# A modulation vector gathered as rows by one product of 512 columns in each feed-forward pass

## The chip, the cores and the metric

The kernel runs on one core of a Trainium2 chip. Its engines are TensorE (PE in the profile), VectorE (DVE), ScalarE (ACT), GpSimd (POOL) and SyncE (SP), which here only issues transfers. The metric is the device time of one execution in microseconds; the median of three runs is given. All times below are in us unless marked ns.

## The reference

Two transformer blocks follow each other on 256 tokens of width 1024. What touches the change:

```python
# first block (twice, around a mixer)
h = h + 0.5 * ((silu(gate) * up) @ w_out)        # gate, up = split(rmsnorm(h) @ w_in); D_FF = 2816
# second block
c_act = silu(c)                                   # c: [1, 1024]
mod = c_act @ w_ada + b_ada                       # w_ada: [1024, 6144]
shift1, scale1, gate1, shift2, scale2, gate2 = split(mod, 6)
h = rms_norm(x, g_pre_mix) * (1.0 + scale1) + shift1
```

The vector `mod` depends on `c` alone. The kernel computes most of it during the two feed-forward stages of the first block, long before it is used.

## The kernel before

**The passes.** Each feed-forward stage (`ffn1`, `ffn2`) goes through its 2816 hidden channels in 11 steps of 256, ten passes of a loop and an end. A pass of TensorE is a wide slab for the gate (48 products of 128x256), a wide slab for the up part (48), and a deep slab (48 products that add to banks 0 to 3). Every weight slab is 128x2048 floats (1 MB), fetched by SyncE into `raw` (three slots). ScalarE copies it into `wh` at reduced precision (the weight copies one, two and three of a pass), and VectorE writes the rest, `raw - wh`, into `wl` (split one, two and three). Three products, `wh` with the high part, `wh` with the low part, `wl` with the high part of the input, make one exact product. Between them VectorE reads the gate bank and the up bank, ScalarE applies the curve (silu), VectorE multiplies, ScalarE rounds the hidden values (`fh`) and VectorE takes their low part (`fl`).

**The modulation.** In each pass one step of 256 of the 6144 columns of `mod` is computed: SyncE fetches 1 MB of `w_ada` into `ada_raw` (L547), GpSimd multiplies it by `c_act` (L692) and folds it three times, 2048 to 1024 to 512 to 256 columns (L695, L697, L701, the last into `ada_sum`). TensorE sums over the partitions by `modulate` (L2175): for each half of `ada_sum` a product with one column of ones, which puts 128 values into one column of bank 7. Ten steps fall into `ffn1`, ten into `ffn2` (`ADA_EARLY` = 20), four into the last stage.

**What sets the order.** Each engine runs its own program in order; semaphores order them among each other. SyncE waits with the fetch of step n for `ada_free`, the third fold of step n-1, and this wait stands ahead of the slabs of the next pass in its queue. TensorE waits for `ada_free` at the end of a pass. Behind `modulate` stands a product of zeros over the gate bank (`long_zeros`, L2151), whose values the next slab's first product overwrites; behind that the loop branches.

At the end of `ffn2` VectorE reads the 40 columns of bank 7 in `modulation_vectors` (L1383 to L1393) and then adds the four banks of the deep slabs to the residual (L1456). ScalarE squares those for the next norms (L1070).

## Time and profile before

| | |
|---|---|
| median of 3 runs | 1006.28 us (1006.11 to 1006.47) |
| the profiled execution | 1004.26 us |
| its span | 1002.4 us, 18812 instructions |
| busy: PE, PEld, DVE, ACT, POOL | 97%, 92%, 78%, 50%, 51% |
| mean traffic | 190 GB/s |

The profile is one execution on the chip. PE's busy share holds modelled ends of pipelined products, so starts are read rather than lengths: 48 products of 256 columns in 5.44 us are 0.113 each, whatever the 278 ns of one record. A VectorE or GpSimd record that is longer than others of its form contains time in which it was blocked after it had been started. In rows of a timeline the bracket gives the idle time before an operation and what ended it.

### The profile page before, as it was taken

The numbers are of one execution on the slowest core, as the hardware profiler recorded it, in microseconds if no ns is written. First come the engines' busy times: TensorE is split into PE (matmuls) and PEld (weight loads), VectorE is DVE, ScalarE is ACT, GpSimd is POOL, SyncE is SP. The second block draws the span as 40 slices with busy tenths as digits, with TensorE's granted clock in tenths as the row PEclk, the third lists the DMA queues.
The fourth block names the chain that finished last, engine by engine and source line by source line (L and its number), as shares of the span: only waits on it lengthen the run. The fifth ranks groups of instructions, "written<-read, shape, count | busy, mean of one in ns | idle before, by whom it ended". The sixth has DMA issues, their size and how long they took to land.

```text
span 1002.4 us, 18812 instructions
## 1 busy us (share of the span) xinstructions
PE 975.8 (97%) x7645; PEld 926.8 (92%) x7645; DVE 779.9 (78%) x810; ACT 501.8 (50%) x587; POOL 511.0 (51%) x302
## 2 busy tenths in 40 slices
PE   9999999999989999999999999999989989999997
PEld 8999999998979899999999999978979979999996
DVE  5776565799995679887787779998978887768764
ACT  7433433477541474434334756667657454343432
POOL 4575767610054037577577699999940104314400
PEclk9999999999998999999999999999989999999999
DMA  8966858747360277686776475572236517675641
GB/s 270 360 211 227 275 194 276 242 129 211 96 198 8 84 224 244 232 270 209 261 241 213 140 194 159 142 216 85 85 109 204 193 50 245 228 247 195 216 161 43
DMA packets 166494, 190.06 MB, mean 190 GB/s; under 512 B 10654, under 2 KB 155628, under 8 KB 166316
## 3 DMA queue, kind: packets, MB, share of 16 engines
q1 hardware_dynamic: 165580, 186.13, 57.1%
q0 software_dynamic: 688, 3.07, 1.1%
q8 instruction: 36, 0.59, 0.2%
q10 hardware_dynamic: 176, 0.15, 0.1%
q14 instruction: 14, 0.11, 0.0%
HBM read 187.17 MB, written 2.16 MB: 189 GB/s over the span
## 4 chain that ended last, share of the span: by engine, by line
PE 73%; DVE 15%; POOL 4%; issue 3%; ACT 2%; SPq 1%; DMA 1%; ACTq 0%; DVEq 0%; POOLq 0%
PE ps L2079 46%; PE ps L2123 11%; PE ps L2131 9%; DVE wl L1348 5%; DVE ps L1756 2%; POOL work L825 2%; POOL con L822 2%; PE ps L2364 1%; PE ps L2310 1%; ACT wh L856 1%; PE ps L2175 1%; SPq L564 1%; POOL work L818 1%; PE ps L2151 1%; PE ps L2235 1%
## 5 line engine op out<-in xcount | busy, mean ns | idle before, releaser
L2079 PE MATMUL ps<-xh,wh 128*128 128x256 f32 x1208 | 340.1, 282 | 6.4 <-DVE work L1375 3.2
L2079 PE MATMUL ps<-xl,wh 128*128 128x256 f32 x1208 | 335.4, 278 | 0.0
L2079 PE MATMUL ps<-xh,wl 128*128 128x256 f32 x1208 | 335.2, 278 | 0.0
L1353 DVE TENSOR_TENSOR wl<-raw,wh 128x2048 fp32r<-128x2048 f32 x78 | 231.5, 2968 | 67.4 <-ACT wh L862 67.1
L2079 PEld LDWEIGHTS ps<-xh,wh 128*128 128x128 f32 x1208 | 228.1, 189 | 12.3 <-issue 7.1
L2079 PEld LDWEIGHTS ps<-xl,wh 128*128 128x128 f32 x1208 | 227.8, 189 | 0.5
L2079 PEld LDWEIGHTS ps<-xh,wl 128*128 128x128 f32 x1208 | 227.5, 188 | 0.0
L862 ACT ACTIVATE wh<-raw 128x2048 fp32r<-128x2048 f32 x78 | 149.9, 1922 | 138.3 <-PE ps L2079 101.4
L1348 DVE TENSOR_TENSOR wl<-raw,wh 128x2048 fp32r<-128x2048 f32 (+1 forms) x72 | 181.5, 2527 | 32.7 <-ACT wh L856 32.0
L692 POOL TENSOR_TENSOR ada_raw<-ada_raw,c_act 128x2048 f32<-128x2048 f32 x24 | 90.6, 3775 | 206.5 <-DMA ada_raw<-in_w_ada 201.3
L856 ACT ACTIVATE wh<-raw 128x2048 fp32r<-128x2048 f32 (+1 forms) x74 | 139.5, 1889 | 59.4 <-PE ps L2079 42.3
L2079 PE MATMUL ps<-yh,wh 128*128 128x256 f32 x480 | 135.7, 283 | 1.2 <-DVE work L1884 0.7
L2079 PE MATMUL ps<-yh,wl 128*128 128x256 f32 x480 | 133.6, 278 | 0.0
L2079 PE MATMUL ps<-yl,wh 128*128 128x256 f32 x480 | 133.5, 278 | 0.0
L2079 PEld LDWEIGHTS ps<-yh,wh 128*128 128x128 f32 x480 | 90.8, 189 | 4.3 <-issue 2.0
L2079 PEld LDWEIGHTS ps<-yl,wh 128*128 128x128 f32 x480 | 91.0, 190 | 0.1
L2079 PEld LDWEIGHTS ps<-yh,wl 128*128 128x128 f32 x480 | 90.7, 189 | 0.0
L2123 PE MATMUL ps<-fh,wl 128*128 128x256 f32 x320 | 88.5, 277 | 0.0
L2123 PE MATMUL ps<-fh,wh 128*128 128x256 f32 x320 | 88.5, 276 | 0.0
L2123 PE MATMUL ps<-fl,wh 128*128 128x256 f32 x320 | 88.5, 276 | 0.0
L695 POOL TENSOR_TENSOR ada_raw<-ada_raw 128x1024 f32<-128x1024 f32 x24 | 82.3, 3427 | 1.9
L697 POOL TENSOR_TENSOR ada_raw<-ada_raw 128x512 f32<-128x512 f32 x24 | 72.4, 3016 | 1.9
(426 smaller groups left out, 1773.0 us busy)
## 6 DMA issues: line engine op xcount, KB each, us to landing
raw<-in_ffn_w_in SPq DMA_DIRECT2D x43, 1024.0 KB, 7.6
ada_raw<-in_w_ada SPq DMA_DIRECT2D x24, 1024.0 KB, 5.1
raw<-in_ffn_w_out SPq DMA_DIRECT2D x22, 1024.0 KB, 6.5
raw<-in_w_in SPq DMA_DIRECT2D x18, 1024.0 KB, 5.3
raw<-in_w_mlp_in SPq DMA_DIRECT2D x16, 1024.0 KB, 5.5
raw<-in_w_mlp_out SPq DMA_DIRECT2D x16, 1024.0 KB, 4.9
raw<-in_w_mix_in SPq DMA_DIRECT2D x14, 1024.0 KB, 5.4
raw<-in_w_mix_out SPq DMA_DIRECT2D x4, 1024.0 KB, 5.2
```

Of the source, the lines that this page charges most:

```text
L692: pool.tensor_tensor(ada_raw[:, :, :], ada_raw[:, :, :], c_act[:, :].unsqueeze(2).to_broadcast([P, KT, 256]), ALU.mult).then_inc(S("ada_pa ...
L695: pool.tensor_tensor(flat[:, 0:1024], flat[:, 0:1024], flat[:, 1024:2048], ALU.add).then_inc(S("ada_part"), 1)
L697: pool.tensor_tensor(flat[:, 0:512], flat[:, 0:512], flat[:, 512:1024], ALU.add).then_inc(S("ada_part"), 1)
L822: ins = pool.tensor_scalar(tap_own[:, n, :], upad[:, t, k:k + T], tap(k, t), 0.0, ALU.mult, ALU.add)
L825: ins = pool.tensor_tensor(sums, sums, tap_own, ALU.add)
L856: act.activation(wh[:, s % SLOTS, 0:n], raw[:, s % SLOTS, 0:n], ACT.Copy).then_inc(high_done, 1)
L862: act.activation(wh[:, s % SLOTS, :], raw[:, s % SLOTS, :], ACT.Copy).then_inc(high_done, 1)
L1348: dve.tensor_tensor(wl[:, s % SLOTS, 0:n], raw[:, s % SLOTS, 0:n], wh[:, s % SLOTS, 0:n].bitcast(F32), ALU.subtract).then_inc(low_done, 1)
L1353: dve.tensor_tensor(wl[:, s % SLOTS, :], raw[:, s % SLOTS, :], wh[:, s % SLOTS, :].bitcast(F32), ALU.subtract).then_inc(low_done, 1)
L2079: mm = pe.matmul(bank[:, m * T:(m + 1) * T], w[:, k, m * P:(m + 1) * P], r[:, k, :], start=(m == 0 and k == 0 and j == 0), stop=(k == KT - ...
L2123: mm = pe.matmul(ps[m // 2][:, (m % 2) * T:(m % 2 + 1) * T], w[:, k, m * P:(m + 1) * P], r[:, k, :], start=(begin and k == 0 and j == 0 an ...
L2131: mm = pe.matmul(ps[n][:, :], r[:, k, tk * P:(tk + 1) * P], w[:, k, half * 512:(half + 1) * 512], start=False, stop=stop, skip_group_check ...
```

## The change

- **Rows instead of columns.** TensorE no longer turns each step into two columns. The step's 256 sums per partition are split into a high part and a low part that stand next to each other (`ada_parts`, 128x512). One product with `step_pick` as weights (128x20, a single column of ones, at the step's place) adds the partition sums to row n of bank 7 and zeros to the 19 others. The bank is cleared once, in `ffn1`. The product of zeros at the end of each pass is gone.
- **GpSimd** folds into another buffer (`ada_fold`: `at_mat` in the first stage, part of `w_v` in the second), then waits for ScalarE and subtracts the high part (128x256). `ada_free` is now this subtraction.
- **ScalarE** makes `step_pick` (128x20) and the high part (128x256) in `high_sum`, which stands between the curve and weight copy two and waits for the third fold.
- **SyncE** waits with the next fetch for the first fold only.
- **At the end of `ffn2`** VectorE copies the 20 rows out, TensorE turns them in `turn_rows` after four of the eight tiles of the last deep slab, and VectorE adds the two parts by reading strided columns in `modulation_vectors`.
- The memset of `qkvp`'s pads moves from the start of GpSimd's program to behind its first loop, since `ada_parts` lies over it. The last stage keeps the old steps (`modulation_late`, `modulate_late`).

TensorE at the end of a loop pass of `ffn1`, before (L2123 is the deep slab, L2175 `modulate`, L2151 the zeros; two records of a small product are one row here):

```order
L2123 MATMUL ps<-fh,wl 128x256
L2175 ISA [waits s_ada_free]
L2175 MATMUL ps<-con,ada_sum 128x1
L2175 ISA
L2175 MATMUL ps<-con,ada_sum 128x1
L2222 REGISTER_ALU
L2151 MATMUL ps<-zero 128x512 [waits s_hidden_gate]
L2226 REGISTER_ALU
L2226 COMPARE_AND_BRANCH
```

The same place after the change (L2168 is the deep slab, L2295 the last one behind the loop):

```order
L2168 MATMUL ps<-fh,wl 128x256
L2219 MATMUL ps<-yl,step_pick 20x512 [waits s_ada_free]
L2286 REGISTER_ALU
L2286 COMPARE_AND_BRANCH
L2295 MATMUL ps<-yl,wh 128x256 [waits low_done,s_hidden_low]
```

Three products and their register work give way to one product, and the wait for `ada_free` stands before it.

ScalarE in a loop pass of `ffn1`, before (L862 the weight copies one, two and three, L891 the curve, L895 the rounding):

```order
L862 ACTIVATE wh<-raw 128x2048 [waits taken]
L890 REGISTER_ALU
L891 ACTIVATE hid<-hid 128x512 [waits s_hidden_gate]
L860 REGISTER_ALU
L861 REGISTER_ALU [waits slot0_loaded]
L862 ACTIVATE wh<-raw 128x2048 [waits taken]
L907 REGISTER_ALU
L895 ACTIVATE fh<-hid 128x512 [waits s_hidden,taken]
L862 ACTIVATE wh<-raw 128x2048 [waits taken,slot1_loaded]
```

And after (L890 the weight copies, L919 the curve, L923 the rounding, L929 and L930 the new ones):

```order
L890 ACTIVATE wh<-raw 128x2048 [waits taken]
L918 REGISTER_ALU
L919 ACTIVATE hid<-hid 128x512 [waits s_hidden_gate]
L928 ISA [waits s_ada_taken]
L929 ISA [waits s_ada_part]
L929 ACTIVATE step_pick<-step_line 128x20
L930 ACTIVATE yl<-work 128x256
L888 REGISTER_ALU
L889 REGISTER_ALU [waits slot0_loaded]
L890 ACTIVATE wh<-raw 128x2048 [waits taken]
L944 REGISTER_ALU
L923 ACTIVATE fh<-hid 128x512 [waits s_hidden,taken]
```

Two waits and two operations have moved in ahead of weight copy two, the rounding and weight copy three.

The diff, cut to its core:

```diff
@@ sync
-            def modulation(step):
-
-                if not isinstance(step, int) or step:
+            def modulation(step, late=False):
+
+                if late:
                     sp.wait_ge(*at("ada_free", step))
+                elif not isinstance(step, int) or step:
+                    sp.wait_ge(*at("ada_part", step * 5 - 3))
@@ gpsimd
+            def modulation(step, name):
+                flat = ada_raw[:, :, :].rearrange("p k m -> p (k m)")
+                fold, parts = ada_fold[name], ada_parts[name]
+                pool.wait_ge(*at("ada_loaded", step * 16 + 16))
+                pool.tensor_tensor(ada_raw[:, :, :], ada_raw[:, :, :], c_act[:, :].unsqueeze(2).to_broadcast([P, KT, 256]),
+                                   ALU.mult).then_inc(S("ada_part"), 1)
+                pool.wait_ge(*at("ada_part", step * 5 + 1))
+                pool.tensor_tensor(fold[:, :], flat[:, 0:1024], flat[:, 1024:2048], ALU.add).then_inc(S("ada_part"), 1)
...
+                pool.tensor_tensor(fold[:, 0:256], fold[:, 0:256], fold[:, 256:512], ALU.add).then_inc(S("ada_part"), 1)
+                pool.wait_ge(*at("ada_part", step * 5 + 5))
+                pool.tensor_tensor(parts[:, 1, :], fold[:, 0:256], parts[:, 0, :].bitcast(F32), ALU.subtract)\
+                    .then_inc(S("ada_free"), 1)
...
+            pool.wait_ge(*at("ada_taken", FF_STEPS - 1))
+            pool.memset(qkvp[:, :, 0:3], 0.0).then_inc(S("pads"), 1)
@@ scalar, ffn
+                def high_sum(step):
+                    if not isinstance(step, int) or step:
+                        act.wait_ge(*at("ada_taken", step))
+                    act.wait_ge(*at("ada_part", step * 5 + 4))
+                    act.activation(step_pick[:, :], step_line[:, bass.ds(step * -1 + (ADA_EARLY - 1), ADA_EARLY)], ACT.Copy)
+                    act.activation(ada_parts[name][:, 0, :], ada_fold[name][:, 0:256], ACT.Copy).then_inc(S("ada_part"), 1)
...
                     silu(i + 2)
+                    high_sum(i + first)
                     cast_in_loop(s + 4, i, 3, 1)
@@ vector, modulation_vectors
                 dve.wait_ge(*at("ada_taken", ADA_EARLY))
+                dve.tensor_copy(ada_rows, ps[7][0:ADA_EARLY, :]).then_inc(S("ada_rows"), 1)
...
+                dve.wait_ge(*at("ada_cols", 1))
...
-                st(dve.tensor_tensor(ada[:, 0:n], ps[7][:, 0:n], vec[:, g * P + r:g * P + r + n], ALU.add))
+                st(dve.tensor_tensor(by_half(ada[:, 0:n]), ps[7][:, 0:n].rearrange("p (m s) -> p m s", m=2),
+                                     by_half(vec[:, g * P + r:g * P + r + n]), ALU.add))
@@ tensor
-            def modulate(step):
+            def modulate(step, name):
+
+                pe.wait_ge(*at("ada_free", step + 1))
+                pe.matmul(ps[7][0:ADA_EARLY, :], step_pick[:, :], ada_parts[name].rearrange("p a t -> p (a t)"), start=False, stop=False, skip_group_check=True)\
+                    .then_inc(S("ada_taken"), 1)
...
+            def turn_rows():
+
+                pe.wait_ge(*at("ada_rows", 1))
+                for half in range(2):
+                    for part in range(2):
+                        mm = pe.matmul(ps[7][:, half * ADA_EARLY:(half + 1) * ADA_EARLY],
+                                       ada_rows[:, part * T + half * P:part * T + (half + 1) * P], ident[0:ADA_EARLY, 0:ADA_EARLY],
+                                       start=(half == 0 and part == 0), stop=(part == 1), skip_group_check=True)
+                mm.then_inc(S("ada_cols"), 1)
@@ tensor, ffn
                     pe.wait_ge(*at("x_in", 4))
+                    long_zeros(ps[7])
                     wide(s0 + 1, up_bank, high, low)
...
-                    modulate(i + (0 if name == "ffn1" else FF_STEPS - 1))
-                    pe.wait_ge(*at(name + "_gate", i + 2))
-                    long_zeros(gate_bank)
+                    modulate(i + (0 if name == "ffn1" else FF_STEPS - 1), name)
...
+                    if name == "ffn2" and m == 3:
+                        turn_rows()
```

## Rows read from the trace of the kernel before

**Rows 1.** Page, part 4: the chain that ended last, by engine.

```profile
PE 73%; DVE 15%; POOL 4%; issue 3%; ACT 2%; SPq 1%; DMA 1%; ACTq 0%; DVEq 0%; POOLq 0%
```

**Rows 2.** Stretches A:B: length, busy PE, PEld, DVE, ACT, POOL, PEclk, DMA, GB/s.

```profile
113.00:130.40 17.40, 17.40 (x150) 16.99 (x150) 11.30 (x7) 6.80 (x6) 11.91 (x4) 1.00 0.71 241
428.70:445.90 17.20, 17.20 (x150) 16.96 (x150) 14.62 (x7) 6.96 (x6) 11.69 (x5) 1.00 0.70 233
```

**Rows 3.** Chain in order of time: start us, us, what.

```profile
43.08 11.10 PE ps L2079 x96
...
124.07 5.44 PE ps L2123 x48
129.51 0.58 PE ps L2175 x4
130.09 0.32 PE ps L2151
...
200.06 5.66 PE ps L2235 x48
...
411.17 0.32 PE ps L2151
...
828.21 5.49 PE ps L2131 x24
```

**Rows 4.** Timeline of PE, ffn2, boundary of a pass: start us, us, what.

```profile
479.44 0.50 PE L2175 MATMUL ps<-con,ada_sum 128*128 128x1 f32 x4
479.87 0.38 PE L2151 MATMUL ps<-zero 1*128 1x512 bf16 x1
480.19 0.38 PE L2079 MATMUL ps<-yh,wh 128*128 128x256 f32 x1
480.41 0.28 PE L2079 MATMUL ps<-yl,wh 128*128 128x256 f32 x1
```

**Rows 5.** Timeline of PE at the loop branch of the last stage.

```profile
855.47 0.50 PE L2175 MATMUL ps<-con,ada_sum 128*128 128x1 f32 x4
...
856.03 0.28 PE L2079 MATMUL ps<-xl,wh 128*128 128x256 f32 x1
```

**Rows 6.** Timeline of POOL, one pass of ffn2.

```profile
427.89 3.61 POOL L692 TENSOR_TENSOR ada_raw<-ada_raw,c_act 128x2048 f32<-128x2048 f32 x1 [5.18 <-DMA ada_raw<-in_w_ada]
431.57 2.73 POOL L695 TENSOR_TENSOR ada_raw<-ada_raw 128x1024 f32<-128x1024 f32 x1
434.38 3.22 POOL L697 TENSOR_TENSOR ada_raw<-ada_raw 128x512 f32<-128x512 f32 x1
437.68 2.67 POOL L701 TENSOR_TENSOR ada_sum<-ada_raw 128x256 f32<-128x256 f32 x1
```

**Rows 7.** Timeline of DVE, the same pass.

```profile
428.72 3.32 DVE L1415 TENSOR_TENSOR fl<-hid,fh 128x512 fp32r<-128x512 f32 x1 [1.25 <-ACT fh L895]
431.96 4.49 DVE L1353 TENSOR_TENSOR wl<-raw,wh 128x2048 fp32r<-128x2048 f32 x1
...
441.78 2.29 DVE L1353 TENSOR_TENSOR wl<-raw,wh 128x2048 fp32r<-128x2048 f32 x1 [1.27 <-ACT wh L862]
```

**Rows 8.** Timeline of SyncE (SPq) and POOL; page, part 6: median to landing.

```profile
402.58 0.37 SPq L541 DMA_DIRECT2D raw<-in_ffn_w_out  x1
...
410.23 3.61 POOL L692 TENSOR_TENSOR ada_raw<-ada_raw,c_act 128x2048 f32<-128x2048 f32 x1 [7.23 <-DMA ada_raw<-in_w_ada]
...
ada_raw<-in_w_ada SPq DMA_DIRECT2D x24, 1024.0 KB, 5.1
```

**Rows 9.** ScalarE's copies by line: busy us, mean ns, idle before.

```profile
L862 ACT ACTIVATE wh<-raw 128x2048 fp32r<-128x2048 f32 x78 | 149.9, 1922 | 138.3 <-PE ps L2079 101.4
...
L1260 ACT ACTIVATE xh<-work 128x256 fp32r<-128x256 f32 x8 | 3.4, 419 | 0.3
```

**Rows 10.** Timeline of DVE and ACT, end of ffn2.

```profile
550.71 0.69 DVE L1456 SCALAR_TENSOR_TENSOR resid<-ps,resid 128x512 f32<-128x512 f32 x1
...
555.62 0.91 ACT L1070 ACTIVATE work<-resid,att_col 128x256 f32<-128x256 f32 x2 [0.46 <-DVE resid L1456]
```

More of the change, by code:

```diff
@@ L447, in two_blocks @@
         y_eps, z_eps, scale_m = kr, kr_raw, ps[6][:, T:2 * T]
+        ada_fold = {"ffn1": at_mat, "ffn2": w_v[:, 0:1024]}
+        ada_parts = {"ffn1": yl[:, 0:2, :], "ffn2": xh[:, 4:6, :]}
+        ada_rows = w_kn[0:ADA_EARLY, 0:512]
         gate_row, z_rows, z_junk = w_qn[:, 0:D], w_kn, w_v
@@ L663, in _ @@
                     deep(s + 1 + i * 6, s + 1, "w_mlp_out_2", i * 3 + r)
-                modulation(i + ADA_EARLY)
+                modulation(i + ADA_EARLY, late=True)
             for k in range(ADA_MLP * SLOTS + 1, MLP_STEPS):
@@ L684, in _, with modulation_late @@
             pool.memset(zero[:, :], 0.0).then_inc(S("zero"), 1)
-            pool.memset(qkvp[:, :, 0:3], 0.0).then_inc(S("pads"), 1)
+            ps_(pool.memset(step_line[:, :], 0.0))
+            ps_.sync()
+            pool.memset(step_line[:, ADA_EARLY - 1:ADA_EARLY], 1.0).then_inc(S("pads"), 1)
             pool.memset(mpad[:, :, 0:2], 0.0).then_inc(S("pads"), 1)
-            def modulation(step):
+            def modulation(step, name):
[6 more added lines that the diff above has]
+                pool.tensor_tensor(fold[:, :], flat[:, 0:1024], flat[:, 1024:2048], ALU.add).then_inc(S("ada_part"), 1)
+                pool.wait_ge(*at("ada_part", step * 5 + 2))
+                pool.tensor_tensor(fold[:, 0:512], fold[:, 0:512], fold[:, 512:1024], ALU.add).then_inc(S("ada_part"), 1)
+                pool.wait_ge(*at("ada_part", step * 5 + 3))
+                pool.tensor_tensor(fold[:, 0:256], fold[:, 0:256], fold[:, 256:512], ALU.add).then_inc(S("ada_part"), 1)
+                pool.wait_ge(*at("ada_part", step * 5 + 5))
+                pool.tensor_tensor(parts[:, 1, :], fold[:, 0:256], parts[:, 0, :].bitcast(F32), ALU.subtract)\
+                    .then_inc(S("ada_free"), 1)
+            def modulation_late(step):
                 flat = ada_raw[:, :, :].rearrange("p k m -> p (k m)")
@@ L693, in modulation @@
                                    ALU.mult).then_inc(S("ada_part"), 1)
-                pool.wait_ge(*at("ada_part", step * 3 + 1))
+                pool.wait_ge(*at("ada_part", step * 3 + 1 + 2 * ADA_EARLY))
                 pool.tensor_tensor(flat[:, 0:1024], flat[:, 0:1024], flat[:, 1024:2048], ALU.add).then_inc(S("ada_part"), 1)
-                pool.wait_ge(*at("ada_part", step * 3 + 2))
+                pool.wait_ge(*at("ada_part", step * 3 + 2 + 2 * ADA_EARLY))
                 pool.tensor_tensor(flat[:, 0:512], flat[:, 0:512], flat[:, 512:1024], ALU.add).then_inc(S("ada_part"), 1)
-                pool.wait_ge(*at("ada_part", step * 3 + 3))
-                if not isinstance(step, int) or step:
-                    pool.wait_ge(*at("ada_taken", step))
+                pool.wait_ge(*at("ada_part", step * 3 + 3 + 2 * ADA_EARLY))
+                pool.wait_ge(*at("ada_taken", step))
                 pool.tensor_tensor(ada_sum[:, :], flat[:, 0:256], flat[:, 256:512], ALU.add).then_inc(S("ada_free"), 1)
@@ L716, in _ @@
             pool.wait_ge(low_done, 3)
-            modulation(0)
+            modulation(0, "ffn1")
             pool.dma_start(con[:, N_CONST_FIRST:N_CONST], a["table"][:, N_CONST_FIRST:]).then_inc(S("con_rest"), 16)
@@ L722, in _ @@
             with pool.Fori(0, FF_STEPS - 2) as i:
-                modulation(i + 1)
+                modulation(i + 1, "ffn1")
+            pool.wait_ge(*at("ada_taken", FF_STEPS - 1))
+            pool.memset(qkvp[:, :, 0:3], 0.0).then_inc(S("pads"), 1)
             def add_pairs(n, ready, src, pairs=range(4)):
@@ L784, in _ @@
             with pool.Fori(0, FF_STEPS - 1) as i:
-                modulation(i + (FF_STEPS - 1))
+                modulation(i + (FF_STEPS - 1), "ffn2")
+            pool.wait_ge(*at("ada_free", ADA_EARLY))
             pool.wait_ge(*at("pos_loaded", 16))
@@ L840, in _ @@
             with pool.Fori(0, ADA_MLP) as i:
-                modulation(i + ADA_EARLY)
+                modulation_late(i + ADA_EARLY)
         @block.scalar
@@ L895, in round_hidden @@
                     act.activation(high[:, :, :], pair(hid[:, 3, :]), ACT.Copy).then_inc(S(name + "_fh"), 1)
+                def high_sum(step):
[4 more added lines that the diff above has]
+                    act.activation(ada_parts[name][:, 0, :], ada_fold[name][:, 0:256], ACT.Copy).then_inc(S("ada_part"), 1)
+                first = 0 if name == "ffn1" else FF_STEPS - 1
                 cast(s0 + 3)
@@ L912, in ffn @@
                 silu(FF_STEPS)
+                high_sum(first + FF_STEPS - 2)
                 round_hidden(FF_STEPS, last_high[name])
@@ L1489, in _ @@
             s0 = FIRST["mix"]
-            dve.wait_ge(*at("pads", 2))
+            dve.wait_ge(*at("pads", 3))
             dve.wait_ge(*at("con_rest", 16))
```

11 lines of the change are left out of this document (8 added, 3 removed).

## The prediction

> **What bounds the kernel now.** I read the chain of waits by engine first. TensorE (PE) carries 73% of it [rows 1], so the question is what TensorE does at the place of the change, and for whom it waits there. Next the stretches of one feed-forward pass (first stage: ffn1, second: ffn2): PE is busy in all of it at the full granted clock, VectorE (DVE) 11.30 us of 17.4 in the first stage and 14.62 us of 17.2 in the second, ScalarE (ACT) under 7, GpSimd (POOL) some 11.9, the DMA engines 0.7 [rows 2]. Then the chain in order of time. A pass is 96 products of the two wide slabs (11.10 us), 48 of the deep slab (5.44), the four small modulation products and one product of zeros [rows 3]. In the first stage the small products take 0.58 and the zeros 0.32. From 43.08 to 200.06 there are nine passes of 17.44 on average (first stage); from the wide start at 411.49 (the end of the zeros) to 480.19 four of 17.18 (second stage) [rows 3, 4]. So the second stage is paced by PE alone, the first waits some 0.25 a pass for GpSimd: its loop of transfer, four vector operations and "free" closes just when the deep slab ends.
>
> **The boundary of a pass.** In the timeline of PE the small products start at 479.44, the zeros 0.43 later, the next wide product 0.32 after that, and its successor 0.22 later instead of the usual 0.113 (5.44 over 48). From 479.44 to 480.41, less one normal spacing, that is 0.86 us without useful streaming, in each of 20 passes [rows 3, 4].
>
> **What the change removes and adds on PE.** It takes away the four small products (0.43) and the zeros (0.43 with the bubble behind them) and puts in one product of 512 columns. A 512-column product of the same type streams in 5.49/24 = 0.23 [rows 3]. For the bubble behind it (the loop branch stands there) I bound from both sides: none, or the same 0.20 as behind the zeros. The last stage of the kernel has the same small products directly before its branch: from 855.47 to 856.03 less one spacing is 0.45, which is the small products alone with no bubble to speak of [rows 5]. There the products last 0.43, here the cover is 0.23, so I take 0.20: boundary 0.43, saving 0.43 a pass. Bounds of the boundary: 0.23 to 0.64. A pass paced by PE alone is then 16.54 + 0.23 + 0.20, about 16.77.
>
> The Trainium skill's page "Runtime: NRT & Kernel Launch", section on instruction fetch mechanics, says that a taken branch to a target outside the fetched window must refetch and stalls. The row of the last stage shows no such stall behind 0.43 of cover; by the rule it could show behind 0.23. That is the upper bound 0.64 and the fourth case below.
>
> **GpSimd's work and the copy of its input.** A step keeps its multiply and three folds, and gains a subtraction of 256 columns. The first fold now writes elsewhere, so the next input may be fetched as soon as that fold is done; SyncE comes to it right behind the deep slab's transfer, no longer at the end of the pass. That transfer follows split three: after the deep slab's end a rounding (about 0.6), copy three (1.92) and the split (2.29), so about 4.8 into a pass [rows 7, 9]. Today the modulation's fetch lands 5.1 after its issue (the median), and 7.65 after the deep slab's issue when it goes behind it (402.58 to 410.23) [rows 8]. From 4.8 this gives 12.5 into the pass, where it was 4.2 into the next (5.1 less the 0.9 of the boundary). So the wait of the first stage's passes for GpSimd should go, unless something else is late. What would be late is the port.
>
> **The operations of VectorE and GpSimd exclude each other.** In the rows of one pass DVE's low part of the hidden values (own time 0.54) is asked for at 428.72 and ends at 432.04, after GpSimd's multiply ended at 431.50. GpSimd's first fold ends at 434.30, DVE's split of a slab, asked for at 431.96, at 436.45, GpSimd's second fold, asked for at 434.38, at 437.60 [rows 6, 7]. From one end to the next the own times are 3.61, 2.26 and 1.15 for POOL, and by halving 0.6 for the third fold; 0.54 and 2.15 for DVE. The readings of PSUM by DVE take no part. Sum a pass now: POOL 7.6, DVE 3 x 2.15 + 2 x 0.54 = 7.5, together 15.1 of 17.19. After: one more operation of 0.6, together 15.7 of 16.77. 1.0 us stays free, and both engines would have to be there to use the rest. They are not: the fold must go through ScalarE before GpSimd can subtract (a copy of 256 columns is 0.42 [rows 9], with the small one of the picking column, estimated at 0.1 by its 20 columns, and two hops some 0.6), and DVE waits about 1.2 a pass for copy three and as much for the rounding [rows 7].
>
> The Trainium skill's page "SBUF — State Buffer", section "SBUF: two separate sides", has this as a lock held for the whole instruction between GpSimd and VectorE operations with two SBUF inputs. By the rule the added subtraction costs VectorE time although GpSimd has idle time (case one); if it did not hold, the sum would be that of case two. The rows agree with the rule.
>
> **What ScalarE's new place costs.** The two copies stand between the curve and weight copy two and wait for the third fold. If GpSimd starts its multiply at 12.5, then with today's total of 12.15 for four contended operations (427.89 to 440.35 with gaps, less 0.3) [rows 6] the third fold ends at 24.6, which is 7.9 into the next pass, before the curve is through (in the pass from 428.7 the first split ends at 436.45 [rows 7], and a reading and the curve follow: 9). No block. But a multiply at 12.5 stands in front of DVE's split of slab two (asked for at 13): that ends at 18.2, the hidden product behind the first fold at 20.9, the rounding, copy three and split three follow at 21.5, 23.4 and 25.7, so 8.9 into the next pass instead of 4.7. The deep slab's fetch is issued there, and the modulation's behind it lands at 16.6 instead of 12.5. The third fold is then through at 12 into the following pass, copy two waits for it (0.9 late), and the subtraction, contended at 2.67, ends at 15.3, only 1.2 before PE asks. One more collision of 1.9 makes PE wait 0.7. Queued behind a waiting high sum are copy two, the rounding and copy three, and behind these DVE's splits.
>
> So the period lies between 16.77 (never late) and 18.1 (POOL's contended 12.15 + 2.67 + 0.6, with hops 15.5, plus the 2.6 that the fetch loses behind the deep slab's, each pass). I take 17.1: one late pass in two, 0.7 each, which is 0.33 on the average.
>
> **The sum.** First stage: nine passes from 17.44 to 17.1, 3.1; its first pass, in which nothing contends, 0.4. Second stage: ten passes from 17.19 to 17.1, 0.9. Added once: a product of zeros for bank 7 at the start, 0.35 [rows 3], and the turn of the rows in the last deep slab. For the turn DVE copies 20x512 (0.69 by its first residual sum, which reads as many columns [rows 10], beside PE's work), PE runs 4 products in two parts each, 8 x 0.11 = 0.9 [rows 4], at 2.7 into the slab, and DVE's modulation vectors wait for it with the residual sums behind them. The first residual sum was at 550.71 [rows 10]; now the turn ends at 552.8, the vectors at 553.6. With residual sums of 0.6 and ScalarE's squares of 0.87 a pair the last square ends at about 558.0 where it was 556.53 [rows 10]: 1.5, less part of what the earlier boundary gives, 1.4. Bounds 0.9 (PE's time alone) to 2.5 (all of the delay of the first sum). GpSimd's later work starts earlier or as before: nothing. The memset of the pads falls in GpSimd's idle time behind the last pass. Total: 3.1 + 0.4 + 0.9 - 0.35 - 1.4 = 2.7 faster. The profiled execution takes 1004.26 (span 1002.4); so 1001.6 for it, and against the median 1006.28, which is 2.0 above the profiled one, 1003.6.
>
> **The rivals.**
> - *Two, the port is no matter* (17%): all passes at 16.77. Nine times 0.67, 0.4, ten times 0.42, less 1.75: 8.9 faster, 997.4. For it: today's second stage loses nothing at 15.1 of 17.19. Against: DVE is blocked there for 2 to 2.8 us at a time.
> - *Three, slower* (23%): the late pass feeds on itself. Place: ScalarE's high sum holds copy two, so split two meets the next multiply. It decides once the subtraction ends more than 16.5 into its pass, from a fetch landing about 17.8. At a period of 17.5: first stage 9 x 0.06 lost, second 10 x 0.31 lost, 1.75 lost, 0.4 won: 5.0 slower, 1011.3. At 18.1 it would be 16 slower.
> - *Four, a bubble behind the product* (10%): boundary 0.64, period 16.98, port harmless: 4.1 + 0.4 + 2.1 - 1.75 = 4.9 faster, 1001.4.
> - *Five, it comes to nothing* (15%): period 17.2 from here and there a late pass; 2.2 + 0.4 - 0.1 - 1.75 = 0.8 faster, 1005.5.
>
> **Chances.** My forecast 35%, its own range 1001.3 to 1005.6 (periods 17.0 to 17.2). A measurement of this kernel tells 0.2%, 2.0 us, from no change. Faster: 60% of mine, two, four, a little of five: 0.50. Slower: 0.24. Same: 0.26. The range reaches into two and three: 997.0 to 1010.5.
>
> **What would show it.** PE's boundary: small products and zeros gone, one 512-column product, the next wide product 0.3 to 0.5 behind its start. GpSimd: multiply 10 to 17 into a pass, no wait for the transfer of some 5 in each pass of the first stage. DVE's busy time up from 11.3 to over 13 in the first stage. ScalarE waiting for GpSimd at the high sum in some passes, none in others. PE waiting for GpSimd's subtraction in some passes: if in none and the passes are 16.8, case two. In the tail the first residual sum some 2.5 later. I am wrong if the passes lengthen everywhere, or if PE waits for a slab's low part instead of the subtraction.

## The result and the profile after

The changed kernel takes 1012.39 (median of 5 runs, 1008.33 to 1015.71), the kernel before 1006.14 beside it (5 runs, 1005.99 to 1006.47): a ratio of 1.0064, 95% interval 1.0044 to 1.0084. It is slower, by more than the 0.2% that can be told apart, and lies above my range. The profiled execution took 1008.33, its span is 1006.5.

Part 4 of its page, by engine, against [rows 1]:

```profile
PE 40%; POOL 24%; DVE 15%; issue 14%; ACT 4%; DMA 1%; POOLq 0%; ACTq 0%; DVEq 0%
```

TensorE no longer carries the chain. A pass is counted here from the start of the one product of 512 columns (L2219) to the next. The boundary itself is better than forecast. Timeline of PE in ffn2 (start us, us, what), against [rows 4]:

```profile
425.01 0.28 PE L2168 MATMUL ps<-fh,wl 128*128 128x256 f32 x1
425.12 0.39 PE L2219 MATMUL ps<-xh,step_pick 128*20 128x512 f32 x1
425.36 0.28 PE L2124 MATMUL ps<-yh,wh 128*128 128x256 f32 x1
```

The next wide product starts 0.24 behind the product of 512 columns, without a bubble: 0.86 of [rows 3, 4] has become 0.24, not 0.43. But only eleven of the eighteen passes between the boundaries have the period that this gives, 16.56. The other seven take 17.17 to 20.68; in ffn1 they come every second time from the fifth pass on, in ffn2 from the third. Here are three passes in a row, against [rows 2] (length, busy PE, PEld, DVE, ACT, POOL, granted clock, DMA share, GB/s):

```profile
109.50:128.10 18.60, 16.90 (x148) 16.62 (x147) 16.64 (x8) 7.28 (x8) 11.81 (x5) 1.00 0.50 168
128.10:144.60 16.50, 16.50 (x147) 16.46 (x145) 11.68 (x7) 6.44 (x7) 12.64 (x5) 1.00 0.92 300
144.60:163.60 19.00, 17.16 (x148) 16.58 (x148) 17.19 (x8) 8.00 (x8) 14.30 (x5) 1.00 0.55 183
```

The clock is full in all three, so these late passes are waits. Of the seven only the longest (180.2 to 200.8, the last of ffn1) has a fall of the clock in it: 0.57 in 194 to 198, in part at the lower level of 1.2 GHz, which is worth some 1.7 of its 20.68 (0.43 of these 4.0). The list of waits (engine, line, for whom: us in total, times, longest):

```profile
ACT step_pick L929 <- POOL work L709: 37.0, 8, 5.3
PE ps L2168 <- DVE wl L1391: 11.1, 7, 1.9
```

ScalarE's high sum waits eight times for GpSimd's third fold, up to 5.3. TensorE waits seven times, as often as there are late passes, and it waits at the deep slab (L2168) for split three (L1391). It does not wait for the subtraction.

**One late pass, link by link** (109.5 to 128.1). ScalarE: the curve L919, the high sum L929 and L930, weight copy two L890, the rounding L923, then copy three:

```profile
101.46 0.63 ACT L919 ACTIVATE hid<-hid 128x512 f32<-128x512 f32 x1 [0.70 <-DVE hid L1413]
107.34 0.22 ACT L929 ACTIVATE step_pick<-step_line 128x20 fp32r x1 [5.25 <-POOL work L709]
...
107.78 1.90 ACT L890 ACTIVATE wh<-raw 128x2048 fp32r<-128x2048 f32 x1
117.69 0.64 ACT L923 ACTIVATE fh<-hid 128x512 fp32r<-128x512 f32 x1 [8.01 <-DVE hid L1456]
118.23 1.90 ACT L890 ACTIVATE wh<-raw 128x2048 fp32r<-128x2048 f32 x1
```

ScalarE was through the curve at 102.1. Copy two has to wait for TensorE to leave its slab, which comes 11.4 into a pass (the first experiment shows it), here at 104.4; it starts at 107.78, held 3.4 by the high sum. GpSimd: third fold, then multiply and first fold of the next step, then the multiply after that:

```profile
106.47 0.74 POOL L709 TENSOR_TENSOR work<-work 128x256 f32<-128x256 f32 x1
...
109.04 3.61 POOL L702 TENSOR_TENSOR ada_raw<-ada_raw,c_act 128x2048 f32<-128x2048 f32 x1 [0.35 <-DMA ada_raw<-in_w_ada]
112.73 4.32 POOL L705 TENSOR_TENSOR work<-ada_raw 128x1024 f32<-128x1024 f32 x1
...
130.89 3.61 POOL L702 TENSOR_TENSOR ada_raw<-ada_raw,c_act 128x2048 f32<-128x2048 f32 x1 [5.02 <-DMA ada_raw<-in_w_ada]
```

VectorE: split two, the hidden product, split three:

```profile
109.71 5.08 DVE L1391 TENSOR_TENSOR wl<-raw,wh 128x2048 fp32r<-128x2048 f32 x1 [3.88 <-ACT wh L890]
114.72 2.88 DVE L1456 TENSOR_TENSOR hid<-hid 128x512 f32<-128x512 f32 x1
...
120.17 2.29 DVE L1391 TENSOR_TENSOR wl<-raw,wh 128x2048 fp32r<-128x2048 f32 x1 [0.86 <-ACT wh L890]
```

Split two comes to VectorE at 109.71, 0.67 after GpSimd's next multiply has started, and takes 5.08 where [rows 7] had 4.49 and its own time is some 2.2. The hidden product behind it takes 2.88 instead of 0.68, because GpSimd's first fold has got in ahead. So the rounding comes at 117.69 and split three ends at 122.46. TensorE at the deep slab:

```profile
120.54 0.28 PE L2124 MATMUL ps<-xh,wl 128*128 128x256 f32 x1
122.51 0.39 PE L2168 MATMUL ps<-fh,wh 128*128 128x256 f32 x1 [1.70 <-DVE wl L1391]
```

And SyncE's queue (L546 the deep slab's fetch, L554 the modulation's):

```profile
101.01 0.37 SPq L546 DMA_DIRECT2D raw<-in_ffn_w_out  x1
103.25 0.37 SPq L554 DMA_DIRECT2D ada_raw<-in_w_ada  x1
...
122.64 0.37 SPq L546 DMA_DIRECT2D raw<-in_ffn_w_out  x1
123.30 0.37 SPq L554 DMA_DIRECT2D ada_raw<-in_w_ada  x1
```

In the pass before, the modulation's fetch went out at 103.25, with the first fold. In the late pass the first fold ended at 117.05, but the fetch stands behind the deep slab's, which has to wait for split three: it goes out at 123.30, 6.2 later, and the multiply starts at 130.89. So the third fold is late again when ScalarE comes to the high sum in the next pass, and everything repeats: one pass in phase, one late. The place of the collision changes a little. In the late pass from 144.6 split two gets in just ahead of the multiply and takes 2.29, the hidden product is held instead (4.09), and then split three (3.39); TensorE waits 1.7 there too.

**Where 4.1 of span went**, from the first wide or deep product behind a boundary to the next such place, both kernels:

| stretch | before | after | difference | forecast |
|---|---|---|---|---|
| start to the first boundary | 43.01 | 43.49 | +0.5 | -0.05 |
| nine passes of ffn1 | 156.98 | 157.58 | +0.6 | -3.1 |
| mixer | 194.23 | 191.16 | -3.1 | 0 |
| nine passes of ffn2 | 154.74 | 156.88 | +2.1 | -0.9 |
| last boundary to glu's wide slab | 12.65 | 16.47 | +3.8 | +1.4 |
| the rest | 440.8 | 440.9 | +0.1 | 0 |

The +0.6 of ffn1 holds the 1.7 of the clock; the waits alone would have left that stage 1.1 shorter than before.

The tail of ffn2 on VectorE and PE (the copy of the 20 rows, the turn, the bias, the first two residual sums), against [rows 10]:

```profile
552.83 0.67 DVE L1423 COPY work<-ps 20x512 f32<-20x512 f32 x1
554.65 0.20 DVE L1431 TENSOR_TENSOR ada<-ps,vec 128x40 f32<-128x40 f32 x1 [1.16 <-PE ps L2241]
...
555.55 0.69 DVE L1501 SCALAR_TENSOR_TENSOR resid<-ps,resid 128x512 f32<-128x512 f32 x1
```
```profile
553.55 1.06 PE L2241 MATMUL ps<-con,work 20*128 20x20 f32 x8 [1.44 <-DVE work L1423]
```

### The profile page after: what moved, and what is told of

Its sections match the earlier page's. It is cut to its first block, busy times and chain, and to the rows that moved or that the text cites. A ratio compares the mean times of both kernels' runs of the same rounds, so it can differ in the third digit from the quotient of the medians.

```text
span 1006.5 us, 18735 instructions
## 1 busy us (share of the span) xinstructions
PE 966.5 (96%) x7574; PEld 918.7 (91%) x7574; DVE 812.4 (81%) x811; ACT 508.9 (51%) x627; POOL 525.1 (52%) x324
## 4 chain that ended last, share of the span: by engine, by line
PE 40%; POOL 24%; DVE 15%; issue 14%; ACT 4%; DMA 1%; POOLq 0%; ACTq 0%; DVEq 0%
PE ps L2124 23%; PE ps L2176 9%; POOL ada_raw L702 6%; POOL work L705 6%; DVE wl L1386 5%; POOL work L707 4%; POOL work L709 3%; POOL work L853 2%; DVE ps L1801 2%; POOL con L850 2%; ACT wh L884 1%; PE ps L2426 1%; ACT wh L890 1%; DMA raw<-in_ffn_w_in 1%; PE ps L2372 1%
## 5 line engine op out<-in xcount | busy, mean ns | idle before, releaser
L1391 DVE TENSOR_TENSOR wl<-raw,wh 128x2048 fp32r<-128x2048 f32 x78 | 244.0, 3129 | 61.1 <-ACT wh L890 60.1
L890 ACT ACTIVATE wh<-raw 128x2048 fp32r<-128x2048 f32 x78 | 148.3, 1909 | 66.7 <-PE ps L2124 61.3
L702 POOL TENSOR_TENSOR ada_raw<-ada_raw,c_act 128x2048 f32<-128x2048 f32 x20 | 74.9, 3747 | 53.0 <-DMA ada_raw<-in_w_ada 47.9
L2168 PE MATMUL ps<-fh,wh 128*128 128x256 f32 x320 | 89.9, 281 | 11.1 <-DVE wl L1391 11.1
L2168 PE MATMUL ps<-fh,wl 128*128 128x256 f32 x320 | 89.3, 279 | 0.0
L2168 PE MATMUL ps<-fl,wh 128*128 128x256 f32 x320 | 89.2, 279 | 0.0
L705 POOL TENSOR_TENSOR work<-ada_raw 128x1024 f32<-128x1024 f32 x20 | 73.4, 3672 | 1.6
L755 POOL TENSOR_TENSOR work<-work 128x256 f32<-128x256 f32 x13 | 12.8, 990 | 113.9 <-ACT work L907 55.0
```

The lines of the kernel that those rows point to most:

```text
L702: pool.tensor_tensor(ada_raw[:, :, :], ada_raw[:, :, :], c_act[:, :].unsqueeze(2).to_broadcast([P, KT, 256]), ALU.mult).then_inc(S("ada_pa ...
L705: pool.tensor_tensor(fold[:, :], flat[:, 0:1024], flat[:, 1024:2048], ALU.add).then_inc(S("ada_part"), 1)
L890: act.activation(wh[:, s % SLOTS, :], raw[:, s % SLOTS, :], ACT.Copy).then_inc(high_done, 1)
L1391: dve.tensor_tensor(wl[:, s % SLOTS, :], raw[:, s % SLOTS, :], wh[:, s % SLOTS, :].bitcast(F32), ALU.subtract).then_inc(low_done, 1)
L2168: mm = pe.matmul(ps[m // 2][:, (m % 2) * T:(m % 2 + 1) * T], w[:, k, m * P:(m + 1) * P], r[:, k, :], start=(begin and k == 0 and j == 0 an ...
```

## The experiments

On this trace three theories stood against each other. P, the place: the high sum holds copy two, so VectorE's splits slip into GpSimd's multiply. F, the fetch: the modulation's fetch is held behind the deep slab's, which waits for the split that slipped. L, the load: the added subtraction fills the port shared by VectorE and GpSimd. P and F were taken as rivals; the first two results together say that both are links of one: **the late pass is a loop through several queues**, and a cut at either link ends it. A fourth possibility, tested last, is that the tail slows the kernel. Each ratio is to the kernel before, run beside it on the same chip.

**The high sum behind weight copy two.**

```diff
-                    high_sum(i + first)
                     cast_in_loop(s + 4, i, 3, 1)
+                    high_sum(i + first)
```

> The changed kernel, with ScalarE's two high-sum copies behind weight copy two instead of ahead of it (in the loop passes; the last pass as it was). Theory P (place): in every second pass ScalarE waited for the third fold (5.25 us at 107.34) with copy two behind it, and so split two met the next multiply; then the late passes go, all passes are 16.6 to 17.0 and the time is 998 to 1002. Rival F (fetch): the lateness comes from the modulation's fetch, which stands behind the deep slab's in SyncE's queue, so a late split three makes the next multiply late wherever the high sum stands; then passes of 18.5 to 19 stay at every second place and the time is 1006 to 1014. Rival L (load): the fifth vector operation fills the port that VectorE and GpSimd share; as F, 1006 to 1014.

999.27 (996.53 to 1003.48), ratio 0.9919 (0.9889 to 0.9949). ScalarE in a pass of ffn2, and its wait:

```profile
432.90 1.92 ACT L890 ACTIVATE wh<-raw 128x2048 fp32r<-128x2048 f32 x1 [1.32 <-PE ps L2124]
434.73 0.20 ACT L929 ACTIVATE step_pick<-step_line 128x20 fp32r x1
```
```profile
ACT step_pick L929 <- POOL work L709: 8.7, 3, 3.2
```

Copy two starts when its slab has come free, the high sum behind it is mostly ready (8.7 of waiting in three passes instead of 37.0 in eight), and PE has no wait for a slab's low part in the two stages. That is as P expected, and F and L had the late passes stay. Fourteen of the eighteen passes take 16.56 to 16.66. The place has a price of its own in the first pass (18.14): there TensorE waits 1.4 for the subtraction. The others are 17.03 and two of 17.2 to 17.3 at a slower pace, of which the last section tells.

**The modulation's fetch ahead of the deep slab's.**

```diff
-                    deep(s + 2 + i * 3, s + 2, w_out, i + (start - 1))
                     modulation(i + (1 if name == "ffn1" else FF_STEPS))
+                    deep(s + 2 + i * 3, s + 2, w_out, i + (start - 1))
```

> The changed kernel, with the modulation's fetch issued ahead of the deep slab's in each loop pass of SyncE instead of behind it. Theory F: the fetch no longer waits for split three, lands some 3 to 5 us earlier, no multiply starts late, the late passes go: 998 to 1003. Theory P: ScalarE still holds copy two whenever the third fold is late, but the fold is late less often: some late passes stay, 1003 to 1009. Theory L: the load of the port is the same, 1006 to 1014.

997.99 (993.0 to 1002.35), ratio 0.9887 (0.9838 to 0.9936). SyncE and GpSimd in a pass of ffn2:

```profile
428.12 0.37 SPq L554 DMA_DIRECT2D ada_raw<-in_w_ada  x1
433.56 0.37 SPq L546 DMA_DIRECT2D raw<-in_ffn_w_out  x1
```
```profile
423.62 4.33 POOL L705 TENSOR_TENSOR work<-ada_raw 128x1024 f32<-128x1024 f32 x1
...
435.13 1.64 POOL L711 TENSOR_TENSOR xh<-work,xh 128x256 fp32r<-128x256 f32 x1 [4.33 <-ACT xh L930]
436.73 3.60 POOL L702 TENSOR_TENSOR ada_raw<-ada_raw,c_act 128x2048 f32<-128x2048 f32 x1
```

The fetch goes out 0.2 after the first fold's end, and the multiply starts right behind the subtraction, in the same place of each pass. The high sum stays where the change put it and, but for one wait of 2.8, holds nothing: periods of 16.56 to 17.19, no late pass. P had expected some late passes to stay (1003 to 1009). So one link cut is enough. In a second run on another chip the same kernel took 998.9, ratio 0.993 (0.9905 to 0.9955):

> The changed kernel with the modulation's fetch issued ahead of the deep slab's, once more, beside the next two on one chip. By the head-of-line theory no late pass (periods 16.57 to 17.2, no wait of TensorE for a slab's low part) and 0.4 to 1.3% faster than before. From the last boundary product to glu's first wide product 15.9, as in its first profile.

Again no late pass (16.5 to 17.2), and the tail from the last boundary's product takes 16.1.

**Without the low part.** No subtraction, one product of 256 columns, so this kernel's modulation has only reduced precision. GpSimd's wait for ScalarE's copy moves to the start of its next step.

```diff
-                pool.wait_ge(*at("ada_part", step * 5 + 5))
-                pool.tensor_tensor(parts[:, 1, :], fold[:, 0:256], parts[:, 0, :].bitcast(F32), ALU.subtract)\
-                    .then_inc(S("ada_free"), 1)
...
-                pe.matmul(ps[7][0:ADA_EARLY, :], step_pick[:, :], ada_parts[name].rearrange("p a t -> p (a t)"), ...
+                pe.matmul(ps[7][0:ADA_EARLY, 0:T], step_pick[:, :], ada_parts[name][:, 0, :], ...
```

> The changed kernel without GpSimd's subtraction: the low part of the modulation's sums is left out, and the product takes 256 columns (the high part alone). GpSimd still waits for ScalarE's copy before the next multiply. Theory L: 0.6 us of port time and a collision of up to 1.9 us go in each pass, so the late passes go: 998 to 1002 with passes of 16.5. Theories P and F: the third fold is as late as before relative to its fetch, late passes stay but are shorter by 0.7 to 2: 1003 to 1009.

1014.35 (1010.63 to 1019.1), ratio 1.0056 (1.0027 to 1.0086): no better than the change itself, far from the 998 to 1002 of L and above the 1003 to 1009 expected by P and F. Its waits (each line number is one lower here, GpSimd's folds two higher):

```profile
ACT step_pick L928 <- POOL work L711: 45.1, 9, 5.5
PE ps L2167 <- DVE wl L1390: 11.3, 7, 1.9
```

Again seven late passes, of 18.1 to 19.2 (five of the others are at 17.08 instead of 16.44, the slower pace). The subtraction isn't what makes them, and my ledger of the port, in which it was the one new entry, could not have shown them: the order of the queues makes them.

**The fetch held to the end of the step**, as before the change, with the high sum ahead of copy two:

```diff
-                    sp.wait_ge(*at("ada_part", step * 5 - 3))
+                    sp.wait_ge(*at("ada_free", step))
```

> The changed kernel, but SyncE waits with each modulation fetch for the subtraction of the step before (as the kernel before waits for its last fold), so each multiply starts 4 to 5 us into a pass and the third fold ends near 16.5. Theory P (place): ScalarE then holds copy two in every pass, not in every second, until about 16.5, and split three comes near its need: late passes everywhere, 17.5 to 19 each, 1010 to 1030. Against it: if only the collision of split two with the multiply matters, the multiply at 4 to 5 does not meet it, and the passes are 16.6 to 17.2: 997 to 1006.

1043.4 (1035.93 to 1044.73), ratio 1.036 (1.0315 to 1.0404). Waits:

```profile
ACT step_pick L929 <- POOL work L709: 95.2, 18, 6.8
PE ps L2219 <- POOL yl L711: 12.6, 9, 2.1
PE ps L2219 <- POOL xh L711: 10.7, 8, 2.0
```

Now the high sum waits in every pass, all passes but one take 18.6 to 19.6, and TensorE does wait for the subtraction, up to 2.1. The time is above the 1010 to 1030 expected, and what paces it is not only the place of the high sum. GpSimd's subtraction and next multiply, and SyncE:

```profile
483.21 0.73 POOL L711 TENSOR_TENSOR xh<-work,xh 128x256 fp32r<-128x256 f32 x1 [0.74 <-ACT xh L930]
489.88 3.60 POOL L702 TENSOR_TENSOR ada_raw<-ada_raw,c_act 128x2048 f32<-128x2048 f32 x1 [5.94 <-DMA ada_raw<-in_w_ada]
```
```profile
484.11 0.37 SPq L554 DMA_DIRECT2D ada_raw<-in_w_ada  x1
```

The fetch goes out 0.2 behind the subtraction, the multiply starts when it has landed, and the next subtraction ends at 503.49, 19.55 after the one before: a closed loop of transfer, folds, ScalarE's copy and subtraction, longer than a pass of TensorE. So this run doesn't price the place alone. It shows what the early fetch is worth, and one thing more: copy two is held in every pass, yet TensorE waits nowhere for a slab's low part, since split two (484.96) is through before the multiply. The hold needs the collision to make a late pass. And where TensorE had idled ahead of the product, the next wide product starts 0.56 to 0.64 behind it, not 0.24; whether that is the branch no run tells.

**Both cures**, and both with a moved tail (the turn behind the last deep slab's end, the modulation's vectors behind the residual sums):

> Both cures together: the changed kernel with the high sum behind weight copy two and the modulation's fetch ahead of the deep slab's. If place and fetch are two links of one loop (late third fold, late copy two, split two behind the multiply, late split three, late fetch, late third fold), then either cut is enough and both together give little more: passes of 16.57, ratio to the kernel before 0.987 to 0.992, as each alone. If they are two causes that add, each alone would have left late passes that the other takes, and the ratio falls below 0.985.

1000.65 (996.18 to 1004.36), ratio 0.9951 (0.9928 to 0.9975), no wait of PE for a low part in the two stages. Two cures bring no more than one, so they don't add: they cut the same loop. The ratio is even above the expected 0.987 to 0.992; in the trace seven of the eighteen passes are at the slower pace (17.2 to 17.3), which may be a part of it; whether the other executions have them is not shown.

```diff
-                    if name == "ffn2" and m == 3:
-                        turn_rows()
                 mm.then_inc(taken, 1)
+                if name == "ffn2":
+                    turn_rows()
@@ vector
                 if name == "ffn2":
+                    modulation_rest()
                     sub(s + 2)
```

> As the one before, and the rows are turned behind the last deep slab instead of in its middle; VectorE makes the modulation vectors behind its four residual sums instead of ahead of them (the copy of the rows stays ahead). In the changed kernel the first residual sum stood behind the turn. If that is what the end of the second stage costs, 1.5 to 2.5 us come back against the kernel with both cures; if the turn is hidden anyway, nothing, and if the vectors now delay the first scaled input, it loses up to 0.8.

998.14 (992.69 to 1006.66), ratio 0.9937 (0.9906 to 0.9968). From the last boundary's product to glu's first wide product it takes 14.15, against 15.4 with both cures alone. The total's gain of 0.14% lies inside the intervals. (Besides what is shown, TensorE waits at its next sums in bank 7 until the vectors have been read; so in the next two kernels.)

**The moved tail on one cure, and on the changed kernel.**

> The same with the turn of the modulation's rows behind the last deep slab and the modulation's vectors behind the residual sums of the second stage. By the profile of the kernel with both cures and this tail (14.15 from the last boundary product to glu's first wide product, against 15.4 without it) 1.2 to 1.8 us faster than the one without, a ratio lower by 0.0012 to 0.0018. If the tail were hidden anyway, the two would be equal.

994.41 (993.1 to 997.09), ratio 0.9895 (0.9871 to 0.9919), beside 0.993 (0.9905 to 0.9955) for the same without the tail; the tail takes 14.8 against 16.1. That is the 1.3 expected; the ratio's step of 0.0035 is more, but the intervals overlap. The vectors now stand behind the residual sums and delay none:

```profile
541.89 0.67 DVE L1423 COPY work<-ps 20x512 f32<-20x512 f32 x1
542.49 1.27 DVE L1508 SCALAR_TENSOR_TENSOR resid<-ps,resid 128x512 f32<-128x512 f32 x2
...
546.77 0.19 DVE L1438 TENSOR_TENSOR ada<-ps,vec 128x40 f32<-128x40 f32 x1
```

> The changed kernel with the moved turn and vectors alone, both the high sum and the fetch left as changed. The late passes stay (every second one 18.5 to 20.7), the tail shortens from 16.7 to about 14.5: 2 us faster than the changed kernel, so 1.002 to 1.006 of before. If the tail rather than the late passes were what made the change slower, this would be clearly faster than before.

1009.89 (1006.49 to 1016.29), ratio 1.0049 (1.0029 to 1.007). The tail takes 13.6 instead of 16.7, and the late passes stay (17.1 to 20.2). Worth some 3 in this stretch of the trace, in the total no more than the intervals hold (1.0049 against 1.0064), and the kernel is still slower than before: the late passes decide the sign. The 20.2 is again a late pass with a fall of the clock in it (0.66 in 543 to 548).

**TensorE's boundary by itself, on the kernel before.** First without the product of zeros:

```diff
-                    pe.wait_ge(*at(name + "_gate", i + 2))
-                    long_zeros(gate_bank)
```

> The kernel before, with the product of zeros at the end of each pass (and its wait for the gate's reading) taken out, and nothing else. If the boundary is the sum of its products, with nothing behind them: the passes of the second stage fall from 17.19 to 16.76, those of the first stage stay near 17.3, since GpSimd's loop of transfer and folds paces them: 4.3 + 1 = 5.3 faster, 1000 to 1002. If the branch needs the cover of the zeros: 2 faster or nothing, 1004 to 1006.

1007.73 (1003.52 to 1011.95), ratio 1.0009 (0.9976 to 1.0043). Its chain in order of time:

```profile
408.12 0.34 PE ps L2175 x4
408.46 11.41 PE ps L2079 x96
419.88 5.65 PE ps L2123 x48
```

The zeros' 0.32 are gone, and the pass takes 17.41 instead of 17.19: the 96 wide products take 11.41 instead of 11.10, the 48 deep ones 5.65 instead of 5.44 [rows 3], 0.003 to 0.004 each. Every pass of ffn2 is so. Neither time that I had expected came (1000 to 1002, or 1004 to 1006). Then zeros of 64 columns in place of 512:

```diff
-                    long_zeros(gate_bank)
+                    pe.matmul(gate_bank[:, 0:64], zero[0:1, 0:P], zero[0:1, 0:64], start=True, stop=True, ...
```

> The kernel before with a product of zeros of 64 columns instead of 512 at the end of each pass. Without that product the boundary fell by 0.43 but all products of the following pass went at 0.118 instead of 0.1133, and the pass stayed at 17.41. Theory T: what stands directly ahead of the slab sets the pace of its weight loads, and any product of that kind restores it; then the passes of the second stage are 16.9 to 17.0 and the time is 2 to 4 below the kernel before. Against it: the zeros helped by the time they give the sequencer at the branch; then 64 columns are too short and the pace stays at 0.118, passes of 17.4, no change.

```profile
497.18 11.53 PE ps L2079 x96
508.71 5.65 PE ps L2123 x48
```

In most passes the pace is back and the boundary shorter: in ffn2 seven passes have 11.10 and 5.44, and six of them take 17.00, the seventh 17.36. But two are at the slow pace all through (shown: 11.53 and 5.65), so that the stage takes 154.7 as before. The total, 1005.36 (1002.02 to 1008.62), ratio 0.9993 (0.9969 to 1.0017), can't be told from before (2 to 4 less was expected if the pace came back). Without zeros nothing was won that could be measured. The product of 512 columns has the shorter boundary and kept the pace in all eleven passes in phase of the changed kernel's trace, though not always in the other kernels (last section).

The best is the changed kernel with the fetch ahead and the moved tail: 1.05% faster than before (interval 0.81 to 1.29%), and against the change, by the ratios 0.9895 and 1.0064, some 1.7%.

## Why the prediction was wrong

- **What bounds the kernel** was right: TensorE, with the boundary as its only loss, and GpSimd's loop in ffn1.
- **The boundary** was right in direction and mis-sized: 0.24 for the forecast 0.43, below it by the whole bubble of 0.20 that I took over from the zeros. My sum of the pass has a slip besides: 16.54 + 0.23 + 0.20 is 16.97; the 16.77 that the forecast goes by is the old 17.19 less the saving of 0.43. The 16.54 was itself too long, since its 11.10 held the 0.11 of the bubble behind the zeros: the 144 products of a pass in phase take 16.33 here. The gain per pass on TensorE is 0.62. Behind the branch no stall is seen in a pass in phase, and case four is out. A pass in phase takes 16.56 (forecast 16.77).
- **The late pass is the step that failed.** "One late pass in two, 0.7 each" had the count nearly right (seven of eighteen) and the price wrong: 18.89 on average, 2.3 above a good pass. The period is 16.56 + 2.33 x 7/18 = 17.47, where I took 17.1; in ffn2 that is already above the old 17.19. (Of the 0.91 above 16.56 some 0.7 is the wait for split three, 0.09 the fall of the clock in one pass of the seven, the rest a slower pace of some products and small gaps.) I let the high sum hold copy two for 0.9, from a third fold 12 into its pass; it ends 14.2 into it (107.21), and copy two is held 3.4 (ScalarE itself idles 5.25). And I priced what comes of it as a wait for the subtraction, with 1.2 in hand. The wait is at another place, for split three, which ends at 12.9 into the pass (122.46) instead of my 8.9, because copy two, split two and the hidden product had slipped first. This is what I had named as showing me wrong.
- **Rival three** (slower, 1011.3 at a period of 17.5, 23%) is what happened, by its place (the high sum holds copy two, split two meets the multiply) and by its price, but not by its point of decision: the subtraction is in time. Its total of 5.0 lost is near the measured 4.1 by luck: the tail cost 2.4 more than I had in it and the mixer gave back 3.1, which no term had. The experiments bear the loop out: with the high sum moved or with the fetch moved TensorE has no wait for a low part. I had every link of it in the text and gave it less than the forecast, since I followed the phase from one late pass and not around the loop: the fetch that goes out behind a slipped deep slab is the reason for the next hold.
- **The port** was not the measure. The rule of the Trainium skill's page "SBUF — State Buffer", section "SBUF: two separate sides", that the one that starts first keeps the lock for its whole instruction, agrees with the trace: VectorE's split, asked for at 109.71, ends at 114.79, 2.1 (its own time) after GpSimd's multiply. But the sum of busy time, with 1 to spare, said nothing on who gets in ahead of whom; the kernel with less load had as many late passes. Rival two is the state of a kernel without the loop: passes of 16.6.
- **The first pass and the start**: +0.5 instead of -0.05. The gain of the first pass came: from its first wide product to the boundary it takes 16.65 instead of 17.17. But it starts 1.0 later (26.84 for 25.84), most of it ahead of the added zeros, where TensorE's first square sums are already 1.25 late (16.58 for 15.33). Why stays open; in the traces of the other variants the first boundary lies anywhere from 43.2 to 45.7.
- **The tail**: 3.8 for 1.4, above my bound of 2.5. The first residual sum is 4.7 later against its boundary (forecast some 2.5): 2.7 of it because the last split ends that much later, and 2.0 for the copy and the turn. The bound had the second and not the first. The late last pass is the smaller part of the 2.7: with the fetch ahead, without a late pass, the last split still ends 2.0 to 2.1 later than before, and the stretch from the product to glu takes 16.0 and 16.1, against 16.7 here and 13.0, from the zeros, before. So most of the slip belongs to the new order itself, in which GpSimd's multiply and folds meet VectorE's last operations; no run takes that apart.
- **The mixer** gave 3.1 back, which no step had: see the last section. Without it the profiled execution would have been 7 slower, nearer to the medians' difference of 6.25. How much of that difference is clock stays open: the mean granted clock went from 0.992 in the profiled execution, the fastest, down to 0.988 in the others, of which no trace shows where.

## What to carry to other kernels

An operation put into an in-order engine is priced by what it waits for when it comes there, not by its 0.6 of work: list what stands behind it and follow the slip through every queue until it comes back to the operation's own input. If the ring closes (here ScalarE's copy, VectorE's split, SyncE's fetch, GpSimd's fold, ScalarE again), a sum of busy times can't price it, and what looks like two rival causes can be two links of it; cut it where it is cheapest, with a fetch issued ahead of one that has to wait for more.

## What the runs showed of the hardware that I had not expected

**Products of 256 columns have two paces at full granted clock.** Nearly always a whole pass goes at 0.113 to 0.116 a product (11.10 over 96, 5.44 over 48) or at 0.118 to 0.120 (11.53 over 96, 5.65 over 48). Directly behind the small float32 products (128x1) it was the slow one in all nine passes of ffn2 and in seven of nine of ffn1; with zeros of 64 columns between, in two of nine of ffn2; with full zeros (before), in none of nine of ffn2 and one of nine of ffn1. Behind the product of 512 columns it was in none of the eleven passes in phase after the change, in four of eighteen with the fetch ahead (one in its second run) and in seven of eighteen with both cures. What stood before is not all of it: the last slab of ffn1 in the kernel before took 5.66 behind full zeros [rows 3], and after the change 5.45. What decides it stays open.

**The granted clock in the mixer differs from one execution to another.** Before, then after (columns as above, clock in the third place from the right):

```profile
300.00:305.00 5.00, 5.00 (x30) 5.00 (x30) 2.01 (x5) 0.00 (x0) 4.82 (x6) 0.61 0.25 83
305.00:310.00 5.00, 5.00 (x34) 5.00 (x34) 2.66 (x3) 0.60 (x1) 4.84 (x3) 0.71 0.00 0
```
```profile
290.00:295.00 5.00, 5.00 (x32) 5.00 (x32) 5.00 (x3) 0.00 (x0) 4.88 (x3) 0.67 0.89 294
300.00:305.00 5.00, 4.49 (x40) 4.52 (x41) 3.37 (x6) 0.00 (x0) 4.82 (x6) 1.00 0.51 172
305.00:310.00 5.00, 4.92 (x43) 4.73 (x43) 4.55 (x5) 0.60 (x1) 4.84 (x4) 1.00 0.00 0
```

The clock stood at its lower level (1.2 GHz) for some 7 of 300 to 310 before, after a stretch with little work for TensorE (2.29 busy of 5 in 285 to 290, 3.31 in 295 to 300). A shorter fall, between 287 and 294, is in both traces (0.74 in 285 to 290 before, 0.67 in 290 to 295 after); after the change it is the only one in the mixer. In the chain 32 of the same products take 5.40 there before and 3.76 after. Of the 3.1 that the mixer gave back this is most (5.40 + 3.45 against 3.76 + 1.84 in the two pieces alone, 3.25). Its place differs from trace to trace: with the fetch ahead it lay at 295 to 305 with 0.50 to 0.52, in the second run of the same kernel at 295 to 302, with 0.53 and 0.79 in the same two windows. A few us of this kind may also be why twelve runs of one kernel spread over 6 to 14.

**It also falls in stages in which TensorE waits, and there it can cost nothing.** With the fetch held to the end of the step, where each pass has 19.1 for some 16.6 of work, the trace has seven short falls in the passes and the tail of the two stages (such as 0.57 in 82 to 86, 0.67 in 543 to 548). A pass with such a fall takes 19.0 to 19.6, one without 18.6 to 19.3 (but for the first of ffn2, 16.56): GpSimd's loop paces both. Where TensorE sets the pace it costs time, as in the last pass of ffn1 after the change (20.68, the other late passes at most 19.0).
